# Sparse attention's value sums made transposed, two heads in column halves, with GpSimd normalising the probabilities before their transposes

## The reference: what is computed

```python
s = jnp.einsum('bqhd,bqkhd->bhqk', qb, kg).astype(jnp.float32)
p = jax.nn.softmax(jnp.where(valid[:, None], s, -jnp.inf), axis=-1)
return jnp.einsum('bhqk,bqkhd->bqhd', p.astype(vg.dtype), vg)
...
o = o.swapaxes(0, 1).reshape(B, S, H * d)
return o @ w_out
```

## Time and profile before

| | us |
|---|---|
| median of 3 runs | 2672.85 (2667.7 to 2673.63) |
| the profiled execution, its own time | 2673.8 |
| its span in the profile | 2672.1 |
| PE busy | 2467.1 (92%) |
| POOL busy | 1100.1 (41%) |
| DVE busy, ACT busy | 863.5 each (32%) |
| the loop of 32 turns | from about 2173 to 2288 in the span |

### The profile page before, as it was taken

One profiled execution on the slowest core, in us unless ns is written; L12 is line 12 of the kernel. 1 busy time (PEld: TensorE's weight loads), 2 busy tenths in 40 slices (PEclk: granted clock), 3 DMA queues, 4 the chain that ended last, 5 costly groups with the idle time before them and its releaser, 6 DMA issues.

```text
span 2672.1 us, 26974 instructions
## 1 busy us (share of the span) xinstructions
PE 2467.1 (92%) x11150; PEld 1979.2 (74%) x11150; DVE 863.5 (32%) x1506; ACT 863.5 (32%) x1258; POOL 1100.1 (41%) x862
## 2 busy tenths in 40 slices
PE   7999999898887999999788779999999879999999
PEld 5888877686664788887576457888886657788887
DVE  3222117453123322201543853102124875420211
ACT  4322224222432422212333434313236235331231
POOL 6444434423631644443243015444454702454443
PEclk9999999989999999999899779999999889999999
DMA  4332222212310232222112002233222200233322
GB/s 134 95 95 95 95 95 79 64 48 95 126 63 16 86 103 95 95 95 95 48 63 79 0 16 87 88 110 95 95 76 66 77 32 17 64 99 101 100 95 79
DMA packets 148731, 210.73 MB, mean 79 GB/s; under 512 B 6136, under 2 KB 117120, under 8 KB 148608
## 3 DMA queue, kind: packets, MB, share of 16 engines
q1 hardware_dynamic: 148608, 209.00, 24.4%
HBM read 206.89 MB, written 2.10 MB: 78 GB/s over the span
## 4 chain that ended last, share of the span: by engine, by line
PE 77%; DVE 14%; ACT 4%; POOL 3%; issue 1%; DMA 1%; SPq 0%; ACTq 0%; POOLq 0%; DVEq 0%
PE ps L1182 23%; PE ps L1184 22%; PE ps L1183 22%; POOL wlo L702 2%; PE ps L1770 1%; PE ps L1236 1%; POOL sq L715 1%; DVE c_work L2428 1%; ACT whi L762 1%; DVE c_best L2427 1%; DVE small L2282 1%; PE ps L1746 1%; PE ps L1522 1%; PE ps L1397 1%; PE ps L1756 1%
## 5 line engine op out<-in xcount | busy, mean ns | idle before, releaser
L702 POOL TENSOR_TENSOR wlo<-raw,whi 128x512 fp32r<-128x512 f32 x776 | 1008.9, 1332 | 1506.1 <-ACT whi L762 1506.1
L1182 PE MATMUL ps<-hh,whi 128*128 128x512 f32 x1576 | 626.9, 398 | 30.2 <-DVE hl L1877 19.1
L762 ACT ACTIVATE whi<-raw 128x2048 fp32r<-128x2048 f32 (+1 forms) x195 | 370.8, 1904 | 769.7 <-DMA raw<-in_mlp_w 327.6
L1183 PE MATMUL ps<-hl,whi 128*128 128x512 f32 x1576 | 619.5, 393 | 0.0
L1184 PE MATMUL ps<-hh,wlo 128*128 128x512 f32 x1576 | 618.7, 393 | 0.0
L1182 PEld LDWEIGHTS ps<-hh,whi 128*128 128x128 f32 x1576 | 299.7, 190 | 107.6 <-issue 37.2
L1183 PEld LDWEIGHTS ps<-hl,whi 128*128 128x128 f32 x1576 | 300.1, 190 | 63.0 <-issue 1.7
L1184 PEld LDWEIGHTS ps<-hh,wlo 128*128 128x128 f32 x1576 | 299.5, 190 | 63.2
L1183 PE MATMUL ps<-gl,whi 128*128 128x512 f32 x864 | 336.3, 389 | 0.0
L1184 PE MATMUL ps<-gh,wlo 128*128 128x512 f32 x864 | 336.3, 389 | 0.0
L1182 PE MATMUL ps<-gh,whi 128*128 128x512 f32 x864 | 336.3, 389 | 0.0
(11 more groups left out here) (383 smaller groups left out, 2575.1 us busy)
## 6 DMA issues: line engine op xcount, KB each, us to landing
raw<-in_mlp_w SPq DMA_DIRECT2D x64, 1024.0 KB, 5.4
raw<-in_ffn_w_gate SPq DMA_DIRECT2D x22, 1024.0 KB, 5.2
raw<-in_ffn_w_up SPq DMA_DIRECT2D x22, 1024.0 KB, 5.1
raw<-in_ffn_w_down SPq DMA_DIRECT2D x22, 1024.0 KB, 4.8
raw<-in_w_in SPq DMA_DIRECT2D x13, 1024.0 KB, 5.2
raw<-in_diff_w_in SPq DMA_DIRECT2D x12, 1024.0 KB, 4.9
raw<-in_xattn_w_kv SPq DMA_DIRECT2D x8, 1024.0 KB, 5.0
raw<-in_dsa_w_in SPq DMA_DIRECT2D x8, 1024.0 KB, 5.0
```

What stands on the lines that cost most here:

```text
L702: nc.gpsimd.tensor_tensor(wlo[i][:, c], raw[i][:, c], whi[i][:, c].bitcast(F32), ALU.subtract).then_inc(s_lo, 1)
L762: nc.scalar.activation(whi[i][:, 0:width(made[0])], raw[i][:, 0:width(made[0])], ACT.Copy)\
L1182: nc.tensor.matmul(dst, w_hi, x_hi, start=start, stop=False)
L1183: nc.tensor.matmul(dst, w_hi, x_lo, start=False, stop=False)
```

## The change

Three things are changed together.

1. **GpSimd normalises.** The softmax's division, done before on the output (c_o), is now done on c_p, ahead of the transposes. For each turn VectorE takes the reciprocal of the two row sums (inverse(p), one instruction of two columns, placed behind the copy of turn p - 1), GpSimd multiplies c_p of both heads by it (two TENSOR_SCALAR of 128 rows by 128 (qt+1) columns), and turn(p) on TensorE waits for that (s_pn) instead of the exponents (s_ce). The four splits of blocks b + 12 to b + 15 are written between these products, behind those of turns 10, 12, 14 and 28.
2. **The value sums are made transposed.** In weigh, a_v is now what is loaded (64 columns for a head) and c_pT what is streamed (128 columns); head a = 0 fills partitions 0 to 63 of bank 6, head a = 1 partitions 64 to 127. The number of products stays 160.
3. **What this makes needless is gone**: rows_out and c_o on VectorE, turn_out's 32 transposes on TensorE. parts(j) reads bank 6, and runs behind mask_min in turn 4 j + 4; weigh of the next pair waits for it (s_chl) where it waited for c_o (s_cor).

```diff
--- before.py
+++ after.py
@@ -317,7 +317,6 @@
         c_s = arena("c_s", [P, 4, S], 64)
         c_p = arena("c_p", [P, 4, S], 48)
         c_pT = arena("c_pT", [P, 4, S], 56)
-        c_o = put("c_o", [P, 2, S], SG)
         o_h = arena("o_h", [P, KT, S], 16, F32R)
         o_l = arena("o_l", [P, KT, S], 32, F32R)
 
@@ -468,6 +467,7 @@
         s_cor = sem("s_cor")
         s_coT = sem("s_coT")
         s_oh = sem("s_oh")
+        s_pn = sem("s_pn")
         s_chl = sem("s_chl")
 
         def col(name, i):
@@ -738,6 +738,15 @@
                 scaled(2, c_rowc, "dsa_q_norm_2")
                 split_to(b + 11)
                 scaled(3, c_rowa, "dsa_k_norm_2")
+                for p in range(32):
+                    nk = P * (p % 4 + 1)
+                    pool.wait_ge(s_cor, p + 1)
+                    for a in range(2):
+                        slot = 2 * (p % 2) + a
+                        nc.gpsimd.tensor_scalar(c_p[:, slot, 0:nk], c_p[:, slot, 0:nk],
+                                                small[:, 24 + slot:25 + slot], None, ALU.mult).then_inc(s_pn, 1)
+                    if p in (10, 12, 14, 28):
+                        split_to(b + {10: 12, 12: 13, 14: 14, 28: 15}[p])
 
             for stage in stages:
                 if isinstance(stage, Pass) and stage.half % 2 == 0:
@@ -1133,9 +1142,7 @@
                         act.wait_ge(s_cs, 2 * p + a + 1)
                         if p >= 2:
                             act.wait_ge(s_cT, 2 * (p - 2) + a + 1)
-                        if j >= 2 and qt == 0 and a == 0:
-                            act.wait_ge(s_cor, j - 1)
-                        slot, k = 2 * (p % 2) + a, 16 + 8 * (j % 2) + 4 * a + qt
+                        slot, k = 2 * (p % 2) + a, 16 + 2 * (p % 2) + a
                         nc.scalar.activation(c_p[:, slot, 0:nk], c_s[:, slot, 0:nk], ACT.Exp,
                                              bias=small[:, slot:slot + 1], scale=-1.0,
                                              accum_out=small[:, k:k + 1]).then_inc(s_ce, 1)
@@ -1749,7 +1756,7 @@
 
                 def turn(p):
                     for a in range(2):
-                        pe.wait_ge(s_ce, 2 * p + a + 1)
+                        pe.wait_ge(s_pn, 2 * p + a + 1)
                         if p:
                             pe.wait_ge((s_cpTa, s_cpTd)[a], p)
                         for kb in range(p % 4 + 1):
@@ -1760,28 +1767,18 @@
                 def weigh(p):
                     j, qt = divmod(p, 4)
                     if qt == 0 and j:
-                        pe.wait_ge(s_cor, j)
+                        pe.wait_ge(s_chl, j)
                     if p == 16:
                         copied(G_V1, 3)
                     for a in range(2):
                         pe.wait_ge((s_cpTa, s_cpTd)[a], p + 1)
-                        c = qt * P + 64 * a
-                        for kb in range(qt + 1):
-                            r = nc.tensor.matmul(ps[:, 6, c:c + 64], c_pT[:, 2 * (p % 2) + a, ts(kb, P)],
-                                                 a_v[:, kb, ts(2 * j + a, 64)], start=kb == 0, stop=kb == qt)
-                        r.then_inc(s_cpv, 1)
-
-                def turn_out(j):
-                    pe.wait_ge(s_cor, j + 1)
-                    if j:
-                        pe.wait_ge(s_chl, j)
-                    if j < ST - V1_EARLY:
-                        copied(G_V1, V1_EARLY + j)
-                    if 4 <= j < 7:
-                        pe.wait_ge(s_x, 8 * upd + 2 * j - 6)
-                    for st in range(ST):
-                        r = nc.tensor.transpose(ps[:, 7, ts(st, P)], c_o[:, j % 2, ts(st, P)], ident[:, :])
-                    r.then_inc(s_coT, 1)
+                    for kb in range(qt + 1):
+                        for a in range(2):
+                            r = nc.tensor.matmul(ps[64 * a:64 * a + 64, 6, ts(qt, P)],
+                                                 a_v[:, kb, ts(2 * j + a, 64)], c_pT[:, 2 * (p % 2) + a, ts(kb, P)],
+                                                 start=kb == 0, stop=kb == qt)
+                            if kb == qt:
+                                r.then_inc(s_cpv, 1)
 
                 def values(st, part):
 
@@ -1809,8 +1806,8 @@
 
                     bb = b + DSA_BLOCKS + n // 4
                     use(bb)
-                    if n % 2 == 0:
-                        pe.wait_ge(s_chl, 4 + n // 2)
+                    if n == 0:
+                        pe.wait_ge(s_chl, 4)
                     if n:
                         pe.wait_ge(s_x, 8 * upd + n)
                     out_tile(bb, n, range(4), 7 if n < 7 else 0)\
@@ -1824,8 +1821,6 @@
                         scores(p + 2)
                     if p:
                         weigh(p - 1)
-                    if p % 4 == 1 and p > 4:
-                        turn_out(p // 4 - 1)
                     if p >= 18 and p % 2 == 0:
                         first_half((p - 18) // 2)
                     f, part = divmod(p - 2, 4)
@@ -1834,7 +1829,6 @@
                 weigh(31)
                 pe.wait_ge(s_cs, 64)
                 first_half(7)
-                turn_out(7)
                 use(b + 14)
                 pe.wait_ge(s_x, 8 * upd + 8)
                 for k in (4, 5, 6):
@@ -1845,7 +1839,6 @@
                     out_tile(b + 14, n, (7,), n).then_inc(s_used if n == 3 else s_down, 1)
                 pe.wait_ge(s_cpTa, 32)
                 pe.wait_ge(s_cpTd, 32)
-                pe.wait_ge(s_cor, 8)
                 use(b + 15)
                 for n in range(4, 8):
                     out_tile(b + 15, n, range(4, 8), n).then_inc(s_used if n == 7 else s_down, 1)
@@ -2455,23 +2448,18 @@
                                                op0=ALU.add, op1=ALU.min,
                                                accum_out=small[:, slot:slot + 1]).then_inc(s_cs, 1)
 
-                def rows_out(j):
-
+                def inverse(p):
+
+                    dve.wait_ge(s_ce, 2 * p + 2)
+                    k = 16 + 2 * (p % 2)
+                    if p >= 2:
+                        dve.wait_ge(s_pn, 2 * (p - 2) + 2)
+                    V.reciprocal(small[:, k + 8:k + 10], small[:, k:k + 2]).then_inc(s_cor, 1)
+
+                def parts(j):
                     dve.wait_ge(s_cpv, 8 * j + 8)
-                    k = 16 + 8 * (j % 2)
-                    dv.link(V.reciprocal(small[:, 32:40], small[:, k:k + 8]))
-                    if j >= 2:
-                        dve.wait_ge(s_coT, j - 1)
-                    inv = small[:, 32:40].rearrange("p (a t) -> p t a", a=2).unsqueeze(3)
-                    V.tensor_tensor(c_o[:, j % 2, :].rearrange("p (t a e) -> p t a e", t=ST, a=2),
-                                    ps[:, 6, :].rearrange("p (t a e) -> p t a e", t=ST, a=2),
-                                    inv.broadcast_to([P, ST, 2, 64]), ALU.mult).then_inc(s_cor, 1)
-                    dve.wait_ge(s_cor, j + 1)
-
-                def parts(j):
-                    dve.wait_ge(s_coT, j + 1)
-                    dv.link(V.tensor_copy(o_h[:, j, :], ps[:, 7, :]))
-                    split_lo(o_l[:, j, :], ps[:, 7, :], o_h[:, j, :], s_chl)
+                    dv.link(V.tensor_copy(o_h[:, j, :], ps[:, 6, :]))
+                    split_lo(o_l[:, j, :], ps[:, 6, :], o_h[:, j, :], s_chl)
 
                 def add_half(n):
 
@@ -2484,23 +2472,23 @@
 
                 mask_min(0)
                 mask_min(1)
+                inverse(0)
                 for p in range(32):
                     nk = P * (p % 4 + 1)
                     dve.wait_ge(s_cT, 2 * p + 2)
                     if p >= 2:
                         dve.wait_ge(s_cpv, 2 * (p - 2) + 2)
                     V.tensor_copy(c_pT[:, 2 * (p % 2) + 1, 0:nk], ps[:, 5, 0:nk]).then_inc(s_cpTd, 1)
+                    if p < 31:
+                        inverse(p + 1)
                     if p < 30:
                         mask_min(p + 2)
                     if p % 4 == 0 and p:
-                        rows_out(p // 4 - 1)
-                    if p % 4 == 1 and p > 4:
                         parts(p // 4 - 1)
                     if p >= 18 and p % 2 == 0:
                         add_half((p - 18) // 2)
-                rows_out(7)
+                parts(7)
                 add_half(7)
-                parts(7)
                 dve.wait_ge(s_x, 8 * upd + 8)
 
             tile = first_tile
```

## The result

The changed kernel takes 2708.07 us in the median of 4 runs (2707.9 to 2719.4), the kernel before 2670.9 in the same comparison: 1.015 times as long, 95% interval 1.0135 to 1.0166. The forecast was 2691, its range 2677 to 2705. The sign was right; the size was 17 us short, and outside the range.

The account below looks back on a forecast made before the run. TensorE's own work bounds the kernel before; afterwards the normalising link sets the plain turns. 17.3 + 1.4 - 4.2 - 1.5 + 1.0 + 4.0 = +18.0 us gave 2691 us, range 2677 to 2705.

Parts of the forecast that it names:

- Step 2: Plain turns 3 to 17: the normalising link through VectorE and GpSimd sets the time, +0.4 us a group, +1.4 us.
- The chain itself: Group of four plain turns: copies, reciprocals, GpSimd products (4.2), transposes, hand-overs and parts, 11.1 us against 10.66 now.
- The first rival: GpSimd's products cost as much as the two-input bound (1.04 us for 512 columns) or more; about 2701 us, chance 0.09.
- step 4: Loop start: turn 0 has no cover for its reciprocal, two products and hand-overs, +1 us.
- step 3: TensorE's saving from cheaper weigh and no c_o work: -4.2 us in turns from 18 on, -1.5 us at the end.
- odd turns: From turn 18 on, the two odd turns of a group follow the link, 5.35 us against TensorE's 3.7, 1.65 more.
- the whole -2.6: Forecast saving, in us, for the two groups with dense products from turn 19 to 27, at -1.3 a group.
- Step 1: Four GpSimd splits delay the products of turns 11, 13, 15 and 29, so TensorE waits; +17.3 us.
- Step 5: TensorE's clock drops after each of the three early stalls, 1.3 us a stall, +4 us.
- The 0.75 for the wait for c_o: TensorE's wait for c_o, 3.0 us in four places, goes away, saving 0.75 us a group.
- The full 2x for weigh: Skill's theoretical speedup for column halves: weigh at 0.057 us a record, which would make the sum 0.5 us lower.
- The rival that it keeps 0.114: Weigh on TensorE gains nothing and stays at 0.114 us a record; time 2701 us, chance 0.07.

Follow-up runs that it names:

- e4: Changed kernel with GpSimd's product in the two-tensor form, the reciprocal broadcast along the row; 2690.8 us, 1.0077 of the kernel before.
- e3: Changed kernel with three of the four blocks converted and split ahead of the loop; 2699.35 us, 1.0103 of the kernel before.
- e6: Changed kernel with matrix products that nobody reads put into TensorE's waits of turns 1 to 17; 2706.45 us, 1.0131 of the kernel before.
- e5: Changed kernel with the normalising products on VectorE and the first three blocks' conversions and splits ahead of the loop; 2666.41 us, 0.9984 of the kernel before.
- e7: Kernel before with only the first three blocks' conversions and splits moved ahead of the loop; 2675.98 us, 1.0018 of the kernel before.
- e11: Changed kernel, normalising on VectorE, three conversions early, their splits during top-k and after the copies of turns 18 and 21; 2664.29 us, 0.9977 of before.
- e15: Same as e11, but the third split held until turn 22's copy on VectorE instead of turn 21's; 2663.93 us, 0.9968 of the kernel before.
- e12: Kernel before with early conversions and the three splits placed as in e11; 2664.79 us, 0.9978 of the kernel before.
- e13: Changed kernel, GpSimd's product in two-tensor form, three conversions early, their splits during top-k and after the products of turns 18 and 22; 2674.84 us, 1.0009.

## Why the prediction missed

- **Step 2 failed**: "0.75 at 512 columns", with "above by a two-input product", 1.04. The bound rested on the sentence "since it reads one tensor rather than two", and no row of before stood behind it. The runs show the contrary, 1.56 against 1.04 for the same columns, and e4, which changes nothing but this form, takes 17.8 of the 22.3 us by which the loop passed the forecast. The chain itself was good to 1.6 us a group: it gives 11.1 + 8.66 - 4.2 = 15.6 at the true price and 12.7 at e4's, and 13.96 and 11.57 were measured. Its small terms were each somewhat high. In turns 3 to 7 of after the hand-overs are 0.03, 0.09 and 0.06 us where it had 0.1 each, parts holds back turn 5's copy by 0.46 (from 2188.17 to 2188.63) where it had 1, and the four copies take 1.6 where it had 1.95. The first rival, products dearer than the bound, had the right mechanism at 0.09, but was priced only at the bound.
- The same price is in **step 4** (the piece to turn 3 is +3.5 in place of +1: TensorE waits 1.65 us in turn 0, and again 0.17 in turn 1 and 1.37 ahead of turn 3), in **step 3's** odd turns, which took back the whole -2.6, and in the piece from 27 to 31. Put into the prediction's own terms it gives about +43 in all, an estimate: 18.0, and 3.5 x 4.46 = 15.6 in step 2, 3.25 x 1.9 = 6.1 in step 3, 2.6 in step 1 and 0.6 in step 4. That is above the 40.3 measured, as the chain was too long. e4, at 1.04, brings the pieces to +1.6, +0.9, +20.6, -2.3, +2.8 and -1.1, the loop to +22.5 and the time to 2690.8. That this is the forecast's 2691 is partly chance, since the forecast had a lower price and a chain that overcounted; but it shows that no second large mechanism was missed.
- **Step 1 held**: the splits stand where forecast, TensorE names c_p on GpSimd, and the idle times are 6.01, 4.98 and 6.87 us. Over turns 7 to 19 the growth beyond the plain turns' (3 x 3.3) is 28.7 - 9.9 = 18.8, against 15.4 + 4.0 - 0.3 = 19.1 for steps 1, 5 and 3 there. e3 gives 17.0 for moving the three splits with their conversions, less than 15.4 + 4.0 and the two waits of 1.46, and the low clock stayed in part.
- **Step 5 held in size, not in cause**: 4.1 us by e6. It had put the low clock behind the three stalls. e4 shows that part. In after the clock is down from 2195 on, ahead of the first split, and in e3 without any of the three, so the stalls are not its only cause, and the dear product most likely has a share in it; that the sum came to 4 is luck.
- **Step 3's price of weigh held** nearly, but its saving a group was too high. Where TensorE is the bound of all four turns it said 16.24 to 12.94, and e5, which has no wait on TensorE in turns 19 to 27, shows 14.17: 2.1 us, not 3.3. Weigh saves 4.6 - 2.8 = 1.8 there (forecast 2.1) and c_o's transposes 0.45. The 0.75 for the wait for c_o is not to be found: the transposes of c_o in the earlier trace rows have no wait before them, and the 3.0 us stand in the row of the weight loads. The net still came near: with e4's product the two groups from 19 to 27 lost 2.3, forecast 2.6, since the chain's terms were too high as well. (The full 2x for weigh would have lowered the sum by 158 x 0.005 = 0.8 us, not by the 0.5 given there.) Of weigh's records the timeline of TensorE in after has:

```profile
2298.60 1.09 PE L1777 MATMUL ps<-c_pT,a_v 128*64 128x128 f32 x16
2299.62 0.50 PE L1189 MATMUL ps<-o_h,whi 128*128 128x512 f32 x1
...
2316.83 2.04 PE L1777 MATMUL ps<-c_pT,a_v 128*64 128x128 f32 x28
2318.80 0.50 PE L1189 MATMUL ps<-o_h,whi 128*128 128x512 f32 x1
```

  That is 1.02 / 16 = 0.064 and 1.97 / 28 = 0.070 us a record, forecast 0.062, before 0.114. The rival that it keeps 0.114 is out.

The Trainium skill's figure in "GPSIMD Engine Reference", section 3.1 (769 ns for 512 elements in a simple loop) isn't what this instruction costs, 1562 ns for 512 columns, and the measurement decides. The Trainium skill, "SBUF — State Buffer", section "SBUF: two separate sides", says that VectorE's fast mode, and its operations with two SBUF inputs, share a port pair with GpSimd that one of them holds for a whole instruction. e7's rows agree, with 0.42 us becoming 1.36 to 1.48.

## What to carry to other kernels

Before a small operation is moved to an idle engine onto a chain of short turns, its price must come from a row of that very form on that engine; "less to read" is no bound. One copy of it in a dead place of the program, profiled, would have given 1.56 us. Then look at what else the engine's queue holds: a 5 us job that was free while nobody waited for GpSimd became three stalls, and moving it early cost 6 us beside VectorE until it was gated. The value sums made transposed do pay a little in the loop where VectorE normalises and the splits are placed: 109.7 us (e11) and 108.2 (e15) against 112.0 with the placing alone (e12). In the whole time that doesn't show: 0.9968 of before for e15 and 0.9978 for e12, with intervals that overlap.

## What the runs showed of the hardware

- GpSimd's TENSOR_SCALAR takes 602, 923, 1242 and 1562 ns for 128 to 512 columns, 530 to 1492 with a constant, and TENSOR_TENSOR with one operand broadcast 399, 613, 826 and 1039.
- VectorE makes the same product in 284 ns (128 columns) to 504 (384) in e5. Beside a split in e11 two of 384 columns took 2.80 us in place of 0.75.
- With waits of 5 to 7 us every second turn the granted clock was 0.53 to 0.68 in the four windows of 10 us from 2205 to 2245 of after. With no wait over 1.4 us it was 0.66 to 0.84 in e3, from 2195 to 2245, and with waits of at most 1.5 us it was 1.00 in all windows from 2185 to 2275 of e13. So the longest wait alone doesn't tell whether the clock holds.
